# First expert pair of a decoder-trunk kernel: the gather writes its rows already turned, and the gates are turned after the first gate product

## The chip, the cores and the metric

The kernel runs on one core of one Trainium2 chip. The metric is the time in microseconds of one execution on the device, as the median of several runs. TensorE (PE) multiplies and turns tiles, VectorE (DVE) and ScalarE (ACT) do elementwise work, SyncE (SP) issues the large transfers. PE reads its operands from the on-chip memory (SBUF) and writes to PSUM, which has eight banks of 128 partitions x 512 float32 values.

## The reference, cut to what matters

One layer over 320 tokens (256 of a prompt, 64 of samples) with 1024 features. A pooling and a delta-rule mixer are followed by an output projection. Then comes a mixture of 32 experts, of which each token takes four, and it is here that the change lies:

```
h = rmsnorm(x, ln_moe)
logits = h @ router_w + router_b ; top 4 of 32 ; gates = softmax(top_vals)
for each expert e, on the rows of its tokens (xb):
    gt  = minimum(xb @ w_gate[e] + b_gate[e], 7)
    up  = clip(xb @ w_up[e] + b_up[e], -7, 7)
    hid = (up + 1) * (gt * sigmoid(1.702 * gt))
    y   = hid @ w_down[e] + b_down[e]
x[token] += gate * y[slot]
```

A gated per-layer product and a final norm end the layer. Everything is float32; the expert weights are 32 x 3 x 4 MB.

## The kernel before

The five engines run programs of their own, written out by hand and tied by semaphores. Before the experts, PE works through three token tiles (0, 2 and 1 in this order): output projection (L1486), turning of the raw rows (`turn_raw`, L1204), router logits (`logits`, L1504), and ranks of the tokens within each expert (L1584 to L1586 for tiles 0 and 2, bank `rkA`; L1621 to L1623 with all tiles, bank `rkB`). DVE picks the top four (`choose`, L2248 to L2258), makes ranks (L2261), and compares them with a counting row to get the selection matrix `Ssel` (`match_first`, L2265): for each token tile a 128 x 128 matrix of ones and zeros, token by slot, 64 slots for each of the two experts of a pair.

The experts go in 16 pairs. Each pair is three products, gate, up and down (`product`, bias by L1693, weights by L1726), whose weights arrive in 2 MB chunks through a ring of eight slots. The products need the gathered rows with features on the partitions (`xgT`). For the first pair this is made in four steps. `gather_half` (L1594) multiplies with `Ssel` stationary and the normed rows `h3` moving, 512 columns at a time, into banks `ga` and `gb`. ACT copies these to `xg` (L844). PE turns them in eight 128 x 128 pieces (L1204, `ht_region` as source) into banks `xta` and `xtb`. DVE scales these with the norm's weights into `xgT` (`scaled_turn`, L2352). All later pairs have their own gather in bf16 parts (L1567), in the middle of the pair before.

Beside this, DVE multiplies the selection with the gates (`Sgat`, L2347), PE turns the result (three L1204 with `u_region`, bank `sgt`) and ACT copies it out (L1034). `keep_busy` (L1615) issues bias products into an unused bank while PE waits. After the first pair's rows are scaled, DVE works out the table of expert order and overflow blocks (L2357 to L2393), splits the normed rows into three bf16 parts with ACT (L2397, L2400, ACT L1094 and L1097), and only then enters the loop over pairs. There it prepares the next pair's selection (L2316, L2321), takes the gate product out of PSUM (L2450) and marks the experts (`mark_expert`, L2325). PE's gather for the second pair waits for that mark (`pair_sel`).

SP issues a chunk when its ring slot is used up. PE counts these with `chunk_used`. The sequence of SP also waits once for the finished table (L646).

In the trace a float32 product of PE with 128 stationary columns is two MATMUL records, each with a weight load (PEld) of its own. A float32 transpose is one record.

## Time and profile before

| | |
|---|---|
| median of three runs | 1200.1 us (1194.87, 1200.41, 1200.1) |
| span of the profiled execution, first to last instruction | 1196.8 us |
| busy: PE, DVE, ACT | 95%, 34%, 18% |
| data moved | 435.16 MB |

The profile gives the span of its own execution; what lies around the span is not told apart. The median of the runs is 3.3 us above it, and the three runs lie 5.5 us apart. A busy share close to 100% of PE doesn't say that PE sets the end: its records reach over waits for weights.

### The profile page before, as it was taken

Reading aid. Unit: us, or ns where it says so; the run is one execution under the profiler, and the core shown is the slowest. Engines: PE = TensorE matmul, PEld = TensorE weight load, DVE = VectorE, ACT = ScalarE, POOL = GpSimd, SP = SyncE. Lnnn points to the kernel's source line nnn. Section 1 sums busy time; section 2 is a strip of 40 time slices with the busy share of each in tenths; the row PEclk is TensorE's granted clock in tenths of the full one; section 3 lists DMA queues with packets and bytes.
Section 4 is the critical chain, followed back from the end, with each engine's and each line's share of the span. In section 5 each row is a group of like instructions: output and inputs, shape, how many; then the busy total and the mean of one; then the engine's idle time right before and its main releaser. Section 6 shows DMA issues by size and latency. Waiting matters only on the chain.

```text
span 1196.8 us, 15386 instructions
## 1 busy us (share of the span) xinstructions
PE 1141.3 (95%) x5919; PEld 485.4 (41%) x5919; DVE 410.9 (34%) x779; ACT 212.6 (18%) x393; POOL 39.7 (3%) x115
## 2 busy tenths in 40 slices
PE   8999999999999999999999998999999999999997
PEld 5677864433333332333333333333333333332333
DVE  5646764743132222131322231313131313130325
ACT  3434332221111011111010101011110101010025
POOL 6002110000000000000000000000000000000000
PEclk9999999899999999999999999999999999999999
DMA  9911539789999999999999999999999999999931
GB/s 306 292 71 71 167 120 338 266 329 421 429 427 428 426 429 428 424 429 427 428 428 429 427 428 426 428 427 429 425 429 429 428 428 429 428 428 425 419 150 45
DMA packets 50603, 435.16 MB, mean 364 GB/s; under 512 B 6861, under 2 KB 14554, under 8 KB 24812
## 3 DMA queue, kind: packets, MB, share of 16 engines
q1 hardware_dynamic: 44425, 430.22, 87.1%
q10 hardware_dynamic: 6123, 4.18, 1.1%
q8 instruction: 37, 0.61, 0.2%
q14 instruction: 18, 0.15, 0.0%
HBM read 429.54 MB, written 4.11 MB: 362 GB/s over the span
## 4 chain that ended last, share of the span: by engine, by line
PE 70%; DMA 20%; DVE 5%; issue 2%; ACT 2%; POOL 0%; SPq 0%; DVEq 0%; ACTq 0%; POOLq 0%
PE ps L1726 40%; DMA ring<-in_w_gate 13%; DMA ring<-in_w_up 7%; PE ps L1289 7%; PE ps L1672 4%; PE ps L1567 3%; PE ps L1204 3%; PE ps L1486 2%; PE ps L1336 1%; PE ps L1693 1%; PE ps L1403 1%; PE ps L1940 1%; PE ps L1917 1%; DVE x_resid L2426 1%; PE ps L1798 1%
## 5 line engine op out<-in xcount | busy, mean ns | idle before, releaser
L1726 PE MATMUL ps<-ring,ht_region 128*64 128x512 f32 (+1 forms) x2152 | 455.9, 602 | 18.5 <-DMA ring<-in_w_gate 16.4
L1726 PEld LDWEIGHTS ps<-ring,ht_region 128*64 128x64 f32 (+1 forms) x2152 | 149.6, 135 | 309.4 <-issue 309.3
L1726 PE MATMUL ps<-ring,q_region 128*64 128x512 f32 (+1 forms) x1088 | 223.5, 594 | 0.3 <-ACT q_region L844 0.3
L1726 PEld LDWEIGHTS ps<-ring,q_region 128*64 128x64 f32 (+1 forms) x1088 | 71.6, 134 | 144.2 <-issue 143.2
L2426 DVE TENSOR_TENSOR x_resid<-ps,x_resid 128x512 f32<-128x512 f32 (+1 forms) x90 | 62.0, 688 | 148.0 <-PE ps L1672 143.8
L2476 DVE SCALAR_TENSOR_TENSOR q_region<-ps,small,u_region 128x1024 f32<-128x1024 f32 x15 | 19.3, 1283 | 222.9 <-ACT u_region L1076 222.9
L1289 PE MATMUL ps<-ht_region,ring 128*128 128x320 f32 x320 | 89.0, 435 | 1.7 <-DVE ht_region L1979 0.9
L2468 DVE TENSOR_SCALAR q_region<-ps 128x1024 f32<-128x1024 f32 x15 | 18.4, 1225 | 167.2 <-PE ps L1726 167.2
L1289 PEld LDWEIGHTS ps<-ht_region,ring 128*128 128x128 f32 x320 | 59.8, 190 | 27.2 <-issue 3.1
L1054 ACT ACTIVATE q_region<-q_region 128x1024 f32<-128x1024 f32 x16 | 16.9, 1056 | 292.2 <-DVE q_region L2450 292.1
L1672 PE MATMUL ps<-u_region 128*128 128x512 bf16 (+1 forms) x180 | 54.7, 385 | 3.1 <-DVE x_resid L2426 0.4
L1076 ACT ACTIVATE u_region<-ps,small 128x1024 bf16<-128x1024 f32 x15 | 16.7, 1114 | 226.9 <-PE ps L1726 226.9
L1051 ACT ACTIVATE ht_region<-ps 128x512 f32<-128x512 f32 x30 | 17.9, 598 | 210.3 <-PE ps L1567 210.3
L2426 DVE TENSOR_TENSOR ht_region<-ps,vecs 128x512 f32<-128x512 f32 x30 | 20.7, 691 | 49.5 <-PE ps L1204 48.4
L1567 PE MATMUL ps<-z_region,u_region 128*128 128x512 bf16 x90 | 34.3, 381 | 0.3 <-DVE ht_region L2325 0.3
L1567 PE MATMUL ps<-hmid,u_region 128*128 128x512 bf16 x90 | 34.1, 379 | 0.0
L1672 PE MATMUL ps<-z_region,u_region 128*128 128x512 bf16 (+1 forms) x90 | 34.1, 379 | 0.0
L1693 PE MATMUL ps<-bias_s,ht_region 96*128 96x512 bf16 x96 | 28.9, 382 | 2.6 <-ACT lmask L1107 2.6
L1672 PEld LDWEIGHTS ps<-u_region 128*128 128x128 bf16 (+1 forms) x180 | 12.2, 101 | 46.7 <-DVE x_resid L2426 30.0
L1486 PE MATMUL ps<-ring,ht_region 128*128 128x512 f32 x64 | 28.9, 596 | 0.0
L2010 DVE SCALAR_TENSOR_TENSOR h_region<-q_region,vecs,h_region 128x256 f32<-128x256 f32 (+1 forms) x72 | 27.7, 385 | 2.6
L1204 PE MATMUL ps<-ident,q_region 128*128 128x128 f32 x128 | 20.6, 302 | 7.9 <-ACT ht_region L1051 6.9
(489 smaller groups left out, 906.7 us busy)
## 6 DMA issues: line engine op xcount, KB each, us to landing
ring<-in_w_gate SPq DMA_DIRECT2D x62, 2048.0 KB, 25.0
ring<-in_w_up SPq DMA_DIRECT2D x62, 2048.0 KB, 21.9
ring<-in_w_down SPq DMA_DIRECT2D x57, 2048.0 KB, 26.4
ring<-in_w_down SPq DMA_DIRECT2D x13, 1024.0 KB, 24.4
ring<-in_w_in SPq DMA_DIRECT2D x4, 2048.0 KB, 17.5
ring<-in_w_out SPq DMA_DIRECT2D x2, 2048.0 KB, 8.5
ring<-in_w_up SPq DMA_DIRECT2D x4, 1024.0 KB, 25.0
ring<-in_w_ple_gate SPq DMA_DIRECT2D x2, 2048.0 KB, 20.6
```

What stands on the lines that cost most here:

```text
L1051: lstep(a.activation(out, PS[:, b, 0:width], ACT.Copy, **total), drained[b], done)
L1204: return nc.tensor.transpose(out, in_, ident[0:n, 0:n])
L1289: last = mm(ps[:, 0:T], w[:, k, (c % 4) * P:(c % 4 + 1) * P], hT[:, k, :], start=(k == 0), stop=(k == KT - 1))
L1486: last = mm(ps, hT[:, k, t0:t0 + n], wo[k][:, hf * 512:(hf + 1) * 512], start=(k == 0), stop=(k == KT - 1))
L1567: last = mm(ps, Sselb[:, t, :], part(t)[:, hf * 512:(hf + 1) * 512], start=(t == 0 and i == 0), stop=(t == NT - 1 and i == 2))
L1672: last_ = mm(ps[0:n, :], slots_turned[:, t0:t0 + n], y[:, hf * 512:(hf + 1) * 512], start=(part == 0), stop=(part == 2))
L1693: mm(PS[:, b0 + hf, :], ind[:, half, :], biases[bias][:, hf * 512:(hf + 1) * 512], start=True, stop=False, skip_group_check=True)
L1726: ins = mm(PS[s0_:s0_ + width, b0 + hf, :], lhs[:, k, s0_:s0_ + width], rows[:, kk, hf * 512:(hf + 1) * 512], start=False, stop=(k == KT - 1),
L2010: ins = v.scalar_tensor_tensor(out=out, in0=col(j), scalar=vec("conv_w", j * QKV_T + c), in1=out, op0=ALU.mult, op1=ALU.add)
L2426: lmark(op(*args), drained[b], done)
L2468: lmark(v.tensor_scalar(ubuf, PS[:, 2:4, :].rearrange("p b f -> p (b f)"), LIMIT, -LIMIT, ALU.min, ALU.max), up_act, pair + 2)
L2476: lmark(v.scalar_tensor_tensor(out=gbuf, in0=y_psum, scalar=slot_gate[:, half:half + 1], in1=y_hi, op0=ALU.mult, op1=ALU.subtract), yrest, ...
```

## The change

It touches the first pair alone. (1) `gather_half` has the normed rows stationary, 128 columns at a time with a step of four, and `Ssel` moving, and writes straight to `xta` and `xtb`. The banks `ga` and `gb`, the copies by ACT and the eight turns go. (2) The turning of the gates moves from ahead of the first gate product to behind it; ACT's copy of it moves behind the bf16 splits, and PE waits for that copy ahead of the first down product. (3) PE waits for `xta` alone ahead of the gate product and for `xtb` at its second half. (4) DVE compares both experts in one instruction, makes the first pair's `ind` columns ahead of the last ranks, and scales `xta` and `xtb` ahead of the two products for `Sgat`. (5) The second `keep_busy` issues two products in place of four.

```diff
@@ -335,7 +335,6 @@
         h3_zero = sem("h3_zero")
-        h_gathered = sem("h_gathered")
         hi_cast = sem("hi_cast")
@@ -463,7 +462,7 @@
-        for n, b in (("ga", 2), ("gb", 3), ("rT11", 1), ("lg1", 0), ("rkB", 4), ("sgt", 5), ("xta", 6), ("xtb", 7)):
+        for n, b in (("rT11", 1), ("lg1", 0), ("rkB", 4), ("xta", 6), ("xtb", 7), ("sgt", 5)):
             use(n, b)
@@ -1028,12 +1027,6 @@
             exponent(1)
-            for hf, nm in enumerate(("ga", "gb")):
-                copy(xg[:, hf * 512:(hf + 1) * 512], bank(nm), nm)
-            is_filled(act, "sgt")
-            step(a.activation(gates_turned[0], bank("sgt")[:, 0:T], ACT.Copy, accum_out=slot_gate[:, 0:1]),
-                 dsem("sgt"), uses["sgt"][1] + 1)
-
@@ -1089,12 +1082,15 @@
                 if t == 0:
-                    act.wait_ge(h_gathered, 1)
+                    is_filled(act, "xtb")
                     act.wait_ge(chunk_used, half_used(1))
...
                 step(a.activation(h_mid[:, t, :], h3[:, t, :], ACT.Copy), mid_cast)
+            is_filled(act, "sgt")
+            step(a.activation(gates_turned[0], bank("sgt")[:, 0:T], ACT.Copy, accum_out=slot_gate[:, 0:1]),
+                 dsem("sgt"), uses["sgt"][1] + 1)
             turn_body(0, first=True)
@@ -1586,15 +1582,17 @@
-            first_banks = [fill("ga"), fill("gb")]
+            first_banks = [fill("xta"), fill("xtb")]
...
                 n = TILES[t][1]
-                last = mm(first_banks[hf], Ssel[0:n, t, :], h3[0:n, t, hf * 512:(hf + 1) * 512],
-                          start=(t == ORDER[0]), stop=(t == ORDER[-1]), skip_group_check=True)
+                for kk in range(RPP):
+                    c0 = hf * RPP * P + kk
+                    last = mm(first_banks[hf][:, kk * P:(kk + 1) * P], h3[0:n, t, c0:(hf + 1) * RPP * P:RPP], Ssel[0:n, t, :],
+                              start=(t == ORDER[0] and kk == 0), stop=(t == ORDER[-1]), skip_group_check=True)
                 if t == ORDER[-1]:
-                    last.then_inc(fsem(("ga", "gb")[hf]), 1)
+                    last.then_inc(fsem(("xta", "xtb")[hf]), 1)
@@ -1612,7 +1610,7 @@
                 for _ in range(n):
-                    mm(bank("xta"), onesb[0:3 * E, :], bias3[:, 0:512], start=True, stop=True)
+                    mm(bank("op10"), onesb[0:3 * E, :], bias3[:, 0:512], start=True, stop=True)
@@ -1622,24 +1620,18 @@
             last.then_inc(fsem("rkB"), 1)
-            keep_busy(4)
+            keep_busy(2)
             pe.wait_ge(v_mark, VM["ssel1"])
...
             gather_rows(1)
-            for hf, nm in enumerate(("ga", "gb")):
-                is_drained(pe, nm)
-                ps = fill(("xta", "xtb")[hf])
-                c0 = hf * RPP * P
-                for k in range(4):
-                    last = tr(ps[:, k * P:(k + 1) * P], xg[:, c0 + k:c0 + RPP * P:RPP])
-                last.then_inc(fsem(("xta", "xtb")[hf]), 1)
-            pe.wait_ge(bias_ready, 16 * 12)
-            pe.nop().then_inc(h_gathered, 1)
-            pe.wait_ge(v_mark, VM["sgat"])
-            ps = fill("sgt")
-            for t in range(NT):
-                last = tr(ps[:, t * P:(t + 1) * P], Sgat[:, t, :])
-            last.then_inc(fsem("sgt"), 1)
+
+            def turn_first_gates():
+
+                pe.wait_ge(v_mark, VM["sgat"])
+                ps = fill("sgt")
+                for t in range(NT):
+                    last = tr(ps[:, t * P:(t + 1) * P], Sgat[:, t, :])
+                last.then_inc(fsem("sgt"), 1)
@@ -1683,6 +1675,9 @@
+                            if first and half == 0:
+                                is_drained(pe, "xta")
+                                return
                             for b in (6, 7):
@@ -1707,6 +1702,8 @@
                                     pe.wait_ge(early_in, 16)
+                                if first and half == 0 and bias == 0 and c == 2:
+                                    is_drained(pe, "xtb")
                                 for kk, hf in (LATE_HALF if final and bias == 2 and c > c0 else IN_ROWS):
@@ -1742,6 +1739,8 @@
                         product(0, 0, xgT, 0, rows_turned)
+                        if first and half == 0:
+                            turn_first_gates()
@@ -1773,6 +1772,8 @@
                                 ins.then_inc(fsem(f"pT{k}"), 1)
+                        if first and half == 0:
+                            is_drained(pe, "sgt")
                         product(2 * CPM, 4, hidT, 2)
@@ -2261,9 +2262,10 @@
-            def match_first(t, e):
-                return v.tensor_scalar(Ssel[:, t, e * CAP:(e + 1) * CAP], iotaf[:, 1:CAP + 1], rank[:, e, t:t + 1], None,
-                                       ALU.is_equal)
+            def match_first(t):
+                return v.tensor_tensor(Ssel[:, t, :].rearrange("p (e s) -> p e s", e=2),
+                                       iotaf[:, 1:CAP + 1].unsqueeze(1).broadcast_to([P, 2, CAP]),
+                                       rank[:, 0:2, t].unsqueeze(2).broadcast_to([P, 2, CAP]), ALU.is_equal)
@@ -2290,8 +2292,8 @@
             drain(ranks(2, bank("rkA")[:, E:2 * E]), "rkA")
-            step(match_first(0, 0)), step(match_first(0, 1)), step(match_first(2, 0))
-            mark(match_first(2, 1), "ssel02")
+            step(match_first(0))
+            mark(match_first(2), "ssel02")
             add_half(1, 1)
@@ -2299,10 +2301,12 @@
             choose(1)
+            for a_ in range(2):
+                step(v.tensor_copy(ind[:, 0, a_ * CAP:(a_ + 1) * CAP], ident3[:, a_:a_ + 1].broadcast_to([3 * E, CAP])),
+                     pair_sel if a_ else None)
             is_filled(dve, "rkB")
             step(ranks(1, bank("rkB")[:, 0:E]))
-            step(match_first(1, 0))
-            mark(match_first(1, 1), "ssel1")
+            mark(match_first(1), "ssel1")
             drain(v.tensor_copy(cnt, bank("rkB")[:, E:2 * E]), "rkB")
@@ -2333,8 +2337,6 @@
-            match, weigh, mark_expert = select(0, (0, 1))
-            step(mark_expert(0)), step(mark_expert(1), pair_sel)
             dve.wait_ge(a_mark, AM["exq1"])
@@ -2342,15 +2344,14 @@
                                  den.unsqueeze(2).broadcast_to([P, NT, E]), ALU.mult))
+            for nm, k0 in (("xta", 0), ("xtb", 4)):
+                is_filled(dve, nm)
+                drain(v.tensor_tensor(*scaled_turn(bank(nm), k0)), nm)
             for a_ in range(2):
...
                 mark(ins, "sgat") if a_ else step(ins)
-            for nm, k0 in (("xta", 0), ("xtb", 4)):
-                is_filled(dve, nm)
-                drain(v.tensor_tensor(*scaled_turn(bank(nm), k0)), nm)
-            is_filled(dve, "sgt")
@@ -2484,6 +2485,7 @@
+            is_filled(dve, "sgt")
             turn_body(0, first=True)
```

In the rows below, those of PE stand ahead of the first gate product, from the last `keep_busy` on. `bias_s,onesb` is `keep_busy`, `h_region,u_region` is the gather with `h3` moving, `ident,ht_region` the turn of `xg`, `ident,u_region` that of the gates. Before:

```order
L1615 MATMUL ps<-bias_s,onesb 128x512 x4
L1594 MATMUL ps<-h_region,u_region 128x512 [waits a_mark,v_mark]
L1594 MATMUL ps<-h_region,u_region 128x512
L1204 MATMUL ps<-ident,ht_region 128x128 [waits drained6,drained2]
L1204 MATMUL ps<-ident,ht_region 128x128 x3
L1204 MATMUL ps<-ident,ht_region 128x128 [waits drained7,drained3]
L1204 MATMUL ps<-ident,ht_region 128x128 x3
L1204 MATMUL ps<-ident,u_region 128x128 [waits bias_ready,drained5,v_mark]
L1204 MATMUL ps<-ident,u_region 128x128 x2
L1693 MATMUL ps<-bias_s,ht_region 128x512 [waits drained3,drained2,drained4,drained1,h3_zero,drained0,g_act,pair_sel]
L1693 MATMUL ps<-bias_s,ht_region 128x512
L1726 MATMUL ps<-ring,ht_region 64x512 [waits chunk_in1,chunk_in0,early_in,drained7,drained6]
```

After:

```order
L1613 MATMUL ps<-bias_s,onesb 128x512 x2
L1592 MATMUL ps<-u_region,h_region 128x128 [waits a_mark,v_mark]
L1592 MATMUL ps<-u_region,h_region 128x128 x7
L1688 MATMUL ps<-bias_s,ht_region 128x512 [waits drained3,drained2,drained4,drained1,h3_zero,drained0,g_act,pair_sel]
L1688 MATMUL ps<-bias_s,ht_region 128x512
L1723 MATMUL ps<-ring,ht_region 64x512 [waits chunk_in1,early_in,chunk_in0,drained6]
```

The gather has four times as many instructions of a quarter of the columns, with the operands exchanged, and the three groups of turns between it and the bias products are gone.

The gates' turn stands on PE between the first gate product (its last rows, from `q_region` and `ring`) and the bias of the first up product. After:

```order
L1723 MATMUL ps<-ring,ht_region 64x512
L1723 MATMUL ps<-q_region,ht_region 64x512
L1200 MATMUL ps<-ident,u_region 128x128 [waits drained5,v_mark]
L1200 MATMUL ps<-ident,u_region 128x128 x2
L1688 MATMUL ps<-bias_s,ht_region 128x512 [waits up_act,y_act]
L1688 MATMUL ps<-bias_s,ht_region 128x512
```

Its wait is now for a product of DVE made long before, and the up product comes behind it.

On DVE, from behind the last tile's comparison to the start of the table (`hmid<-hmid,iotaf`). Before:

```order
L2325 CAST ht_region<-ident 96x64 [waits drained4]
L2325 CAST ht_region<-ident 96x64 [waits v_step]
L2339 TENSOR_TENSOR hmid<-hmid,selb 128x96 [waits a_mark,pair_sel]
L2340 TENSOR_REDUCE hmid<-hmid 128x3 [waits v_step]
L2341 TENSOR_SCALAR hmid<-hmid 128x3 [waits v_step]
L2342 RECIPROCAL hmid<-hmid 128x3 [waits v_step]
L2343 TENSOR_TENSOR gate<-hmid 128x3x32 [waits v_step]
L2347 TENSOR_TENSOR u_region<-u_region,gate 128x3x64 [waits v_step] x2
L2352 TENSOR_TENSOR ht_region<-ps,vecs 128x512 [waits filled6,v_mark]
L2352 TENSOR_TENSOR ht_region<-ps,vecs 128x512 [waits filled7,drained6]
L2357 SCALAR_TENSOR_TENSOR hmid<-hmid,iotaf 128x32 [waits ssm_stored,filled5,drained7]
```

After, from that comparison (now one instruction) on:

```order
L2266 TENSOR_TENSOR u_region<-iotaf,rank 128x128 [waits v_step]
L2310 COPY hmid<-ps 128x32 [waits v_mark]
L2341 TENSOR_TENSOR hmid<-hmid,selb 128x96 [waits a_mark,drained4]
L2342 TENSOR_REDUCE hmid<-hmid 128x3 [waits v_step]
L2343 TENSOR_SCALAR hmid<-hmid 128x3 [waits v_step]
L2344 RECIPROCAL hmid<-hmid 128x3 [waits v_step]
L2345 TENSOR_TENSOR gate<-hmid 128x3x32 [waits v_step]
L2349 TENSOR_TENSOR ht_region<-ps,vecs 128x512 [waits filled6,v_step]
L2349 TENSOR_TENSOR ht_region<-ps,vecs 128x512 [waits filled7,drained6]
L2352 TENSOR_TENSOR u_region<-u_region,gate 128x3x64 [waits drained7]
L2352 TENSOR_TENSOR u_region<-u_region,gate 128x3x64 [waits v_step]
L2358 SCALAR_TENSOR_TENSOR hmid<-hmid,iotaf 128x32 [waits ssm_stored,v_mark]
```

The two casts (`mark_expert`) are gone from here to a place ahead of the last ranks, and the two `u_region<-u_region,gate` products (`Sgat`) went behind the two scalings (`ht_region<-ps,vecs`), which the table follows.

## Rows read from the trace of the kernel before

**Rows 1.** The page: the span, and the transfer rate in 40 slices.

```profile
span 1196.8 us, 15386 instructions
...
GB/s 306 292 71 71 167 120 338 266 329 421 429 427 428 426 429 428 424 429 427 428 428 429 427 428 426 428 427 429 425 429 429 428 428 429 428 428 425 419 150 45
```

**Rows 2.** The chain in order of time, late in the span: start, us, what.

```profile
658.27 29.42 DMA ring<-in_w_gate
```

**Rows 3.** Busy time by stretch; the last two columns are DMA share and GB/s.

```profile
218.00:225.00 7.00, 6.85 (x28) 3.18 (x28) 4.12 (x16) 1.72 (x4) 0.00 (x0) 0.82 0.03 12
...
266.00:270.00 4.00, 4.00 (x22) 1.41 (x20) 0.00 (x0) 0.00 (x0) 0.00 (x0) 1.00 0.58 184
270.00:1140.00 870.00, 834.13 (x3962) 298.92 (x3961) 224.12 (x325) 94.49 (x139) 0.00 (x0) 0.99 1.01 427
```

**Rows 4.** PE in order of time, 205 to 223 us: start, us, what, idle before.

```profile
205.37 1.96 PE L1486 MATMUL ps<-ring,ht_region 128*128 128x512 f32 x4
207.64 1.10 PE L1594 MATMUL ps<-h_region,u_region 128*128 128x512 f32 x2 [0.31 <-issue]
208.57 0.60 PE L1204 MATMUL ps<-ident,x_resid 128*128 128x128 f32 x4
...
211.94 2.10 PE L1594 MATMUL ps<-h_region,u_region 64*128 64x512 f32 x4
213.98 1.04 PE L1615 MATMUL ps<-bias_s,onesb 96*128 96x512 bf16 x2
...
215.02 1.87 PE L1615 MATMUL ps<-bias_s,onesb 96*128 96x512 bf16 x4
216.68 3.62 PE L1594 MATMUL ps<-h_region,u_region 128*128 128x512 f32 x4
220.09 1.71 PE L1204 MATMUL ps<-ident,ht_region 128*128 128x128 f32 x8
221.63 0.49 PE L1204 MATMUL ps<-ident,u_region 128*128 128x128 f32 x3
222.09 0.59 PE L1693 MATMUL ps<-bias_s,ht_region 96*128 96x512 bf16 x2
222.70 0.61 PE L1726 MATMUL ps<-ring,ht_region 128*64 128x512 f32 x1
```

**Rows 5.** The same view: a float32 product and a strided turn of this shape.

```profile
175.33 1.05 PE L1336 MATMUL ps<-q_region 128*128 128x128 f32 x8
...
256.28 1.22 PE L1204 MATMUL ps<-ident,q_region 128*128 128x128 f32 x8 [0.52 <-ACT ht_region L1051]
```

**Rows 6.** Stretches of 1 us; the column ahead of the last two is the granted clock.

```profile
213.00:214.00 1.00, 1.00 (x4) 0.12 (x3) 0.86 (x5) 0.21 (x1) 0.00 (x0) 0.84 1.00 426
...
220.00:221.00 1.00, 0.91 (x5) 0.62 (x3) 0.00 (x0) 0.60 (x1) 0.00 (x0) 0.75 0.00 0
```

**Rows 7.** DVE in order of time.

```profile
206.10 1.12 DVE L2265 TENSOR_SCALAR u_region<-iotaf,rank 128x64 f32<-128x64 f32 x4
207.44 0.69 DVE L2220 TENSOR_TENSOR x_resid<-ps,x_resid 128x512 f32<-128x512 f32 x1 [0.21 <-PE ps L1486]
...
215.52 0.55 DVE L2265 TENSOR_SCALAR u_region<-iotaf,rank 128x64 f32<-128x64 f32 x2
...
218.09 0.75 DVE L2347 TENSOR_TENSOR u_region<-u_region,gate 128x192 f32<-128x192 f32 x2
...
221.90 0.69 DVE L2352 TENSOR_TENSOR ht_region<-ps,vecs 128x512 f32<-128x512 f32 x1 [0.20 <-PE ps L1204]
222.63 0.19 DVE L2357 SCALAR_TENSOR_TENSOR hmid<-hmid,iotaf 128x32 f32<-128x32 f32 x1
...
247.46 0.36 DVE L2316 TENSOR_TENSOR u_region<-iotaf,rank 128x192 bf16<-128x192 f32 x1 [1.59 <-issue]
```

**Rows 8.** ACT in order of time, the second copy of the gathered rows.

```profile
220.40 0.60 ACT L844 ACTIVATE ht_region<-ps 128x512 f32<-128x512 f32 x1 [1.11 <-PE ps L1594]
```

**Rows 9.** PE in order of time, at the second pair's gather.

```profile
251.38 0.39 PE L1567 MATMUL ps<-z_region,u_region 128*128 128x512 bf16 x1 [0.30 <-DVE ht_region L2325]
```

## The prediction

> **What bounds the kernel now.** I read the page first: from slice 10 on, the transfer rate stands at 417 to 430 GB/s to the end of the weights [rows 1]. The stretches say the same: full from 270 us to 1140 us at 427 GB/s, half idle at 266 to 270 us and all but idle at 218 to 225 us [rows 3]. Late in the span the chain of work runs for 29.42 us at a time through transfers of weights [rows 2]: PE has used up what the ring held and waits. So the last two thirds of the kernel go at the pace of the transfers. Nothing in the change moves a byte, and it can bring only as much as the stream as a whole starts earlier. The stream is not full until 270 us because its issues wait for ring slots, which PE frees in the first pair. What counts is when PE does the first pair's products, above all the down product behind [rows 9], which frees the slots whose refill ends the last hole.
>
> Next I read PE, DVE and ACT in order of time, from 205 us to the first product and on to the second pair's gather. Here PE has hardly a gap, but much of what it does on the way is there to wait: from 220.09 us, where PE is through with the gather's columns, a chain runs over the tail of the last record (ACT starts 0.31 us later), ACT's copy of 0.60 us [rows 8], four turns, and DVE's scaling, to the first weight product at 222.70 us [rows 4]. That is 2.61 us from 220.09 us. The other chain is DVE's. It starts the expert table at 222.63 us [rows 7] and has work without a pause until it marks the second pair. PE comes to its gather at 251.38 us after 0.30 us of waiting for DVE [rows 9]. **So two chains end together there, PE's at 251.08 us and DVE's at 251.38 us, and a gain counts only as far as both move.**
>
> **Ahead of the last tile.** Four comparisons of 64 columns take 1.12 us, and PE stands 0.31 us ahead of its first gather [rows 4, 7]. Two comparisons of 128 columns: one of 64 is 0.28 us, one of 192 is 0.36 us [rows 7]; I take 0.32 us, so the pair takes 0.64 us plus a little and the gather starts up to 0.4 us earlier. The turns of the raw rows behind it wait for DVE's add, which ends at 208.13 us either way [rows 7], so of their 208.57 us only 0.2 us can go. The bounds are 0 and 0.4 us.
>
> **The gather with its operands exchanged.** Before, one tile and half is two records of 512 columns, and the next work of PE starts 0.93 us after the first (207.64 to 208.57 us, the opening load included [rows 4]); the last tile's records, at half clock, are 0.85 us apart, so at full clock a record is 0.43 us. Now it is four products of two records, 128 columns each. The same view has both sides of the price: eight records of such a product with whole rows stationary take 1.05 us in all, of which 0.28 us is the last one's own length: 0.77 / 7 = 0.11 us a record. Eight turns with stationary columns four apart, as here, take 1.22 us with one break among them, likewise at most 0.94 / 7 = 0.13 us a record [rows 5]. I take 0.12 us, so 0.96 us for eight records, where two old ones took 0.86 us (bounds 0.89 and 1.07 us). The streamed columns are the same number, and only the weight loads could show. The first tile's second half lies under a wait for DVE's copy and costs nothing; should that cover go, it is 0.1 us. Tile 2, 16 records, goes to 1.92 us; before, 211.94 to 213.98 us is 2.04 us, since the clock halves in the last 0.3 us of it (granted clock 0.84 over 213 to 214 us, level 1.2 in place of 2.4 GHz) [rows 4, 6]. PE had products and loads without a gap over 0.31 us before it fell [rows 4]. Started 0.2 us earlier, the tile ends at 213.66 us, 0.3 us earlier.
>
> The Trainium skill (TensorE: Matmul & The Clock Gate, "The mechanism") says that a weight load overlaps with a product in flight only when it goes to other row groups. By that, all 48 loads of the new form would stand in the open and the time would be that of the third rival below; by the rows it stays as summed here. The eight contiguous records disagree, since 0.11 us holds nothing beyond the streaming; the strided ones come near it.
>
> **The last tile.** The two `keep_busy` products and the ranks keep their length, so the ranks are in PSUM 0.3 us earlier. DVE's selection was ready at 216.07 us (215.52 plus 0.55 us [rows 7]); now one comparison of 0.32 us in place of 0.55 us gives 215.54 us. DVE's two casts went ahead of the ranks, into a wait of DVE for PE; if that wait were gone they would cost some 0.4 us. PE issued four fillers from 215.02 us and came to the gather at 216.68 us, 1.66 us for four; two take 0.83 us from 214.72 us, so the selection now decides, and the gather starts at about 215.65 us, **1.0 us earlier**. At half clock it took 216.68 to 220.09 us, 3.41 us [rows 4]. The same columns stream at the same clock, and a record of 0.21 us hides the load better than one of 0.11 us: again 3.41 us, ending at 219.06 us.
>
> **From the gather to the products.** Four turns a half, ACT's copies and a DVE step drop out of the chain. `xta` is filled halfway through the gather, and DVE, through with the gates by then, scales it in 0.69 us under the other half. PE goes on with the two bias products, 0.83 us at half clock (by the fillers), and the weight product starts at about 219.9 us in place of 222.70 us. Until the clock is back at 220.5 us (granted clock 0.75 over 220 to 221 us [rows 6]) it does 0.3 us of work in 0.6 us. In work done PE is 2.5 us ahead. The turn of the gates, 221.63 to 222.09 us, 0.46 us [rows 4], is now behind the gate product and comes back: PE reaches the second gather **2.0 us earlier**, at 249.05 us. `xtb` is needed at the gate product's second half, 7 us in, and is there. ACT's copy of the turned gates stands behind the splits and is wanted only at the down product, many us later: nothing. The moved turn frees no slot and moves no transfer; behind it in PE's queue is the up product, which loses its 0.46 us, counted above.
>
> **DVE.** `xtb` is filled 0.31 us behind the gather's last column, as the old bank was [rows 4, 8]: 219.06 + 0.31 = 219.37 us. Scaling 0.69 us, then the two products for `Sgat`, 0.75 us [rows 7], which before lay hidden under the waiting, and the table starts at about 220.85 us with its step between instructions: **1.75 us earlier** than 222.63 us. What follows is the same work, the next pair's selection included, and SP's wait for the table moves with it. So DVE releases the gather at 251.38 − 1.75 = 249.63 us, after PE's 249.05 us; PE waits 0.6 us there in place of 0.30 us, and DVE's number counts.
>
> **Sum.** The second gather and all behind it, the down product, the slots, and the stream from its last hole on, come 1.75 us earlier, and the end with them. The profiled span of 1196.8 us [rows 1] becomes 1195.05 us. The median of the runs shown, 1200.1 us, is 3.3 us above that span; I take this as what lies around it and carry it over: 1198.3 us. The three runs lie 5.5 us apart, so a measurement of this kernel can hardly tell less than 0.5%, 6 us, from no change.
>
> **The rivals.**
> *The clock stays up.* The fall at 213.68 us follows the logits and a gather of 64 rows, and the change gives PE other records there. Without it the fillers, ranks and last gather (213.98 to 220.09 us, 5.0 us of it streaming) would shrink: the selection would come at about 214.8 us, the gather end at 216.8 us and the table start at 218.6 us: 4 us earlier, 1196.1 us. For it speaks only that every gather record now has a load beside it; against it, that the stretch before the fall stays nearly as it was.
> *The clock stays down longer.* The gather streams ones and zeros from `Ssel` where it streamed the rows. If the half clock lasts 3.4 us longer (as long as half the present stay), PE loses 1.7 us in the products, arrives only 0.3 us earlier, and the end is 1199.8 us.
> *The other side: strided loads don't hide.* If each of the 48 records showed its load for 0.1 us or more beyond my 0.12 us, the 40 that lie on the path cost 4 us and the end is 1202.4 us. It decides from 1.75 / 40 = 0.044 us a record on. The strided turns' 0.13 us at most speaks against it; but those streamed an identity with one record to a turn.
> *Nothing passes on.* If the stream's full part doesn't shift with the first pair, because its last hole is closed by something else, 1200.1 us. Against it: the hole at 266 to 270 us is PE's slots.
>
> **How the numbers follow.** Forecast 1198.3 us, its own range 1197.4 to 1199.2 us, 0.58. Clock up 0.12, clock down longer 0.12, nothing passes on 0.12, loads in the open 0.06. All centres but the last lie between 1196.1 and 1200.1 us; the medians' own spread adds some 3 to 4 us on the lower side, where one of the three runs lay, and 2 on the upper: 1192.5 to 1202 us. Faster by over 0.5% needs 1194.1 us, beyond even the clock case, and can come only together with low runs: 0.15. Slower by over 0.5% needs 1206.1 us: 0.04. Within: 0.81.
>
> **What would show it.** PE: 48 gather records, 0.12 us apart at full clock and 0.21 us at half; gather of the last tile from 215.6 to 219.1 us; first weight product at about 219.9 us; three turns behind the gate product; 0.6 us of waiting for DVE at the second gather at 249.6 us. DVE: table from 220.9 us. Stream: the hole at 266 us at 264.3 us. Wrong would be a granted clock that falls at another time, records over 0.16 us apart, or an end that doesn't follow the second gather.

## The result, and the profile after

The changed kernel takes **1202.04 us** (median of 20 runs, 1199.08 to 1206.02), the kernel before 1198.59 us (20 runs beside it, 1194.08 to 1204.77). The ratio is 1.0031, interval 1.0020 to 1.0043: slower by 0.3%, where 1198.3 us and a ratio of 0.9985 were forecast. By the forecast's own bound of 0.5% this is "within"; the sign is the other one, and the time is that of the rival "strided loads don't hide", which had 0.06. One run of them all (of e9 below, 1218.53 us) was in a slow state and counts in no ratio and no mean.

The profiled execution took 1206.02 us. The page of the changed kernel:

```profile
span 1204.5 us, 15429 instructions
...
GB/s 318 252 95 70 166 114 285 257 358 375 425 427 427 428 428 428 428 426 428 428 427 430 427 427 426 427 430 428 429 427 429 429 429 427 427 428 426 419 152 45
```

What lies around a span is therefore 1.5 us, not the 3.3 us taken from the median; with it the profiled execution of before took 1198.3 us, not 1200.1 us. The span is 7.7 us longer than in [rows 1], but most of that is no work of the change. PE in order of time, from where the rows of [rows 4] begin to the second gather of [rows 9]:

```profile
210.70 1.96 PE L1482 MATMUL ps<-ring,ht_region 128*128 128x512 f32 x4
212.50 1.92 PE L1592 MATMUL ps<-u_region,h_region 128*128 128x128 f32 x8
...
214.69 2.03 PE L1592 MATMUL ps<-u_region,h_region 128*128 128x128 f32 x8
...
218.35 4.10 PE L1592 MATMUL ps<-u_region,h_region 64*128 64x128 f32 x16
...
223.42 1.01 PE L1613 MATMUL ps<-bias_s,onesb 96*128 96x512 bf16 x2
224.27 4.10 PE L1592 MATMUL ps<-u_region,h_region 128*128 128x128 f32 x16
228.17 0.91 PE L1688 MATMUL ps<-bias_s,ht_region 96*128 96x512 bf16 x2
229.00 0.64 PE L1723 MATMUL ps<-ring,ht_region 128*64 128x512 f32 x1
...
242.89 0.55 PE L1200 MATMUL ps<-ident,u_region 128*128 128x128 f32 x3
...
258.98 0.39 PE L1563 MATMUL ps<-z_region,u_region 128*128 128x512 bf16 x1 [1.23 <-DVE ht_region L2329]
```

The first row stood at 205.37 us in [rows 4]. Nothing ahead of it was changed, and over the 18 profiles of this study it stands anywhere from 205.37 us to 210.70 us (the changed kernel again, in e10: 208.84 us). From here on I count all times from this record, which takes those 5.33 us out. Then the first weight product starts at 18.3 us in place of 17.3 us, and the second gather at 48.3 us in place of 46.0 us, 2.3 us later. A late gather record is what [rows 5] did not show: 16 of them take 4.10 us, and single ones lie 0.233 us apart.

DVE in order of time, which answers to [rows 7]:

```profile
211.44 0.62 DVE L2266 TENSOR_TENSOR u_region<-iotaf,rank 128x128 f32<-128x128 f32 x2
...
226.61 0.69 DVE L2349 TENSOR_TENSOR ht_region<-ps,vecs 128x512 f32<-128x512 f32 x1 [0.84 <-PE ps L1592]
228.48 0.69 DVE L2349 TENSOR_TENSOR ht_region<-ps,vecs 128x512 f32<-128x512 f32 x1 [1.17 <-PE ps L1592]
229.21 0.75 DVE L2352 TENSOR_TENSOR u_region<-u_region,gate 128x192 f32<-128x192 f32 x2
229.99 0.19 DVE L2358 SCALAR_TENSOR_TENSOR hmid<-hmid,iotaf 128x32 f32<-128x32 f32 x1
```

DVE waits for the gather twice, 0.84 and 1.17 us, and the table starts at 19.3 us in place of 17.3 us. Stretches of 1 us and of the stream, the answers to [rows 6] and [rows 3]:

```profile
218.00:219.00 1.00, 1.00 (x7) 0.96 (x6) 0.42 (x2) 0.85 (x3) 0.00 (x0) 0.77 0.96 410
...
228.00:229.00 1.00, 1.00 (x4) 0.25 (x3) 0.52 (x1) 0.00 (x0) 0.00 (x0) 0.61 0.07 16
229.00:230.00 1.00, 1.00 (x7) 0.43 (x8) 0.90 (x4) 0.00 (x0) 0.00 (x0) 1.00 0.00 0
272.00:280.00 8.00, 8.00 (x40) 2.59 (x37) 0.00 (x0) 0.00 (x0) 0.00 (x0) 1.00 0.65 246
280.00:1140.00 860.00, 824.29 (x3883) 295.84 (x3883) 223.98 (x325) 93.94 (x138) 0.00 (x0) 0.99 1.01 427
```

The clock falls about where it did but stays down 10.2 us (218.5 to 228.8 us), where it was 6.8 us. The stream is full again from 280 us, at the same 427 GB/s. The last expert weight product starts 941.6 us from the counted record, before 939.3: in this pair of profiles the 2.3 us of the second gather are there at the end.

### The profile page after: what moved, and what is told of

The parts are those of the page before. It is cut to its first block, busy times and chain, and to the rows that moved or that the text cites. A ratio compares the mean times of both kernels' runs of the same rounds, so it can differ in the third digit from the quotient of the medians.

```text
span 1204.5 us, 15429 instructions
## 1 busy us (share of the span) xinstructions
PE 1148.9 (95%) x5945; PEld 496.0 (41%) x5945; DVE 410.8 (34%) x776; ACT 211.5 (18%) x391; POOL 39.2 (3%) x115
## 4 chain that ended last, share of the span: by engine, by line
PE 67%; DMA 21%; DVE 6%; ACT 2%; issue 2%; SPq 1%; POOL 0%; DVEq 0%; ACTq 0%; POOLq 0%
PE ps L1723 40%; DMA ring<-in_w_gate 18%; PE ps L1285 7%; PE ps L1664 4%; PE ps L1563 3%; DMA ring<-in_w_up 2%; PE ps L1200 2%; PE ps L1482 2%; PE ps L1332 2%; PE ps L1688 1%; DVE x_resid L2427 1%; PE ps L1918 1%; PE ps L1592 1%; SPq L604 1%; PE ps L1473 1%
## 5 line engine op out<-in xcount | busy, mean ns | idle before, releaser
L1723 PE MATMUL ps<-ring,ht_region 128*64 128x512 f32 (+1 forms) x2152 | 456.1, 603 | 18.3 <-DMA ring<-in_w_gate 17.8
L2477 DVE SCALAR_TENSOR_TENSOR q_region<-ps,small,u_region 128x1024 f32<-128x1024 f32 x15 | 19.3, 1284 | 222.9 <-ACT u_region L1069 222.9
L2469 DVE TENSOR_SCALAR q_region<-ps 128x1024 f32<-128x1024 f32 x15 | 18.4, 1225 | 165.6 <-PE ps L1723 165.5
L2427 DVE TENSOR_TENSOR ht_region<-ps,vecs 128x512 f32<-128x512 f32 x30 | 20.8, 692 | 49.5 <-PE ps L1200 48.4
## 6 DMA issues: line engine op xcount, KB each, us to landing
ring<-in_w_gate SPq DMA_DIRECT2D x62, 2048.0 KB, 24.6
ring<-in_w_up SPq DMA_DIRECT2D x62, 2048.0 KB, 21.8
```

Of the source, the lines that this page charges most:

```text
L1723: ins = mm(PS[s0_:s0_ + width, b0 + hf, :], lhs[:, k, s0_:s0_ + width], rows[:, kk, hf * 512:(hf + 1) * 512], start=False, stop=(k == KT - 1),
L2427: lmark(op(*args), drained[b], done)
L2469: lmark(v.tensor_scalar(ubuf, PS[:, 2:4, :].rearrange("p b f -> p (b f)"), LIMIT, -LIMIT, ALU.min, ALU.max), up_act, pair + 2)
L2477: lmark(v.scalar_tensor_tensor(out=gbuf, in0=y_psum, scalar=slot_gate[:, half:half + 1], in1=y_hi, op0=ALU.mult, op1=ALU.subtract), yrest, ...
```

## The experiments

Times of the middle columns are counted from the same record, in each kernel's one profile: "last gather" is the first gather record of the last tile, "product" the first weight product, "table" the start of DVE's table, "2nd gather" the second pair's, with what PE waited for it. "Clock down" is how long the clock was down in this stretch; "half clock" is the mean over a kernel's timed runs of the whole time at 1.2 GHz, from each run's granted clock as 2 x (1 - clock) x time. Each ratio is to the kernel before on the same chip.

| kernel | ratio, interval | median us | last gather | product | table | 2nd gather (PE waits) | clock down | half clock |
|---|---|---|---|---|---|---|---|---|
| before | 1 | 1198.59 | 11.3 | 17.3 | 17.3 | 46.0 (0.3) | 6.8 | 21.2 |
| changed | 1.0031 (1.0020, 1.0043) | 1202.04 | 13.6 | 18.3 | 19.3 | 48.3 (1.2) | 10.2 | 26.9 |
| e1 | 0.9984 (0.9968, 1.0000) | 1195.69 | 9.9 | 12.3 | 13.7 | 43.0 (1.9) | none | 18.9 |
| e2 | 0.9981 (0.9964, 0.9999) | 1196.49 | 9.9 | 12.3 | 13.7 | 43.0 (1.9) | none | 20.3 |
| e3 | 0.9998 (0.9981, 1.0015) | 1198.39 | 10.3 | 16.3 | 17.3 | 46.5 (1.5) | 6.8 | 21.8 |
| e5 | 1.0031 (1.0012, 1.0050) | 1201.82 | 13.7 | 17.2 | 18.5 | 47.5 (1.5) | 6.8 | 28.2 |
| e6 | 1.0011 (0.9992, 1.0031) | 1198.26 | 10.3 | 15.2 | 16.0 | 45.0 (1.1) | 6.8 | 24.2 |
| e7 | 1.0026 (1.0005, 1.0046) | 1201.60 | 13.7 | 18.4 | 19.4 | 47.1 (0) | 10.2 | 27.2 |
| e8 | 0.9970 (0.9950, 0.9990) | 1195.40 | 11.0 | 15.0 | 16.2 | 43.7 (0) | 6.8 | 22.7 |
| e9 | 1.0030 (1.0010, 1.0049) | 1199.65 | 12.9 | 15.3 | 16.6 | 45.9 (1.8) | none | 21.4 |
| e10 | 1.0032 (1.0015, 1.0050) | 1200.98 | 13.6 | 18.3 | 19.3 | 48.6 (1.5) | 10.2 | 25.6 |
| e11 | 1.0005 (0.9985, 1.0025) | 1199.07 | 10.2 | 14.6 | 14.5 | 43.1 (0.2) | none | 22.4 |
| e12 | 0.9986 (0.9970, 1.0001) | 1194.70 | 10.2 | 13.3 | 14.6 | 42.3 (0.2) | 3.4 | 21.3 |
| e13 | 1.0029 (1.0011, 1.0046) | 1201.11 | 13.7 | 18.0 | 19.1 | 48.4 (1.7) | 6.8 | 26.6 |
| e14 | 1.0018 (0.9998, 1.0037) | 1200.39 | 12.9 | 15.3 | 16.6 | 45.9 (1.8) | none | 21.4 |
| e15 | 0.9996 (0.9975, 1.0017) | 1196.81 | 9.9 | 12.5 | 13.7 | 42.9 (1.7) | none | 24.2 |
| e16 | 0.9997 (0.9975, 1.0018) | 1198.37 | 9.9 | 12.3 | 13.7 | 42.9 (1.8) | none | 24.6 |

(Before's half clock is that of 134 runs beside e1, e5, e10 and e16; the means of these four sets are 23.3, 21.3, 18.4 and 22.2 us.)

**e1 and e16: contiguous columns.**

```diff
-                    c0 = hf * RPP * P + kk
+                    c0 = hf * RPP * P + kk * P
-                    ... h3[0:n, t, c0:(hf + 1) * RPP * P:RPP], Ssel[0:n, t, :],
+                    ... h3[0:n, t, c0:c0 + P], Ssel[0:n, t, :],
```

> The changed kernel, with the normed rows' stationary columns taken 128 side by side instead of four apart (the first pair's rows then come out with their features in another order, so the first pair multiplies them with the wrong weight rows; the same instructions otherwise). Theory A, the strided weight load is what costs: a record falls from 0.233 us to about 0.11 us at full and 0.21 us at half clock; from the first record of the last four of the output projection to the start of the expert table it takes about 15.5 to 16.5 us (19.29 us changed, 17.26 us before), the second pair's gather follows that, and the time is 0.1 to 0.2% under the kernel before (ratio 0.998 to 0.999). Theory B, the longer stay at half clock costs, whatever the loads do: the records get shorter at full clock, but the half clock still stands for 10 us and the time stays at a ratio of 1.001 to 1.003. Theory C, the first pair passes nothing on to the end: the ratio stays 1.003 whatever the first pair does.

> All gather columns contiguous (first pair's features in a mixed order), again, on this chip: 5 us less than the strided-early kernel, mean half clock 19 to 21 us; ratio to the kernel before 0.998.

PE of e1 in order of time:

```profile
207.18 1.10 PE L1592 MATMUL ps<-u_region,h_region 128*128 128x128 f32 x8
...
211.75 2.05 PE L1592 MATMUL ps<-u_region,h_region 64*128 64x128 f32 x16
...
215.31 2.05 PE L1592 MATMUL ps<-u_region,h_region 128*128 128x128 f32 x16 [0.39 <-DVE u_region L2266]
217.20 0.60 PE L1688 MATMUL ps<-bias_s,ht_region 96*128 96x512 bf16 x2
```

Same instructions, same count, only the addresses differ: at full clock 8 records take 1.10 us where the changed kernel's took 1.92 us. The last tile's 16 take 2.05 us in place of 4.10 us, but there the clock is another one too (up here, down in the changed kernel). The loss is gone. e16 had the same profile but a ratio of 0.9997: what contiguous columns bring over the kernel before is between 0 and 0.2%. Of what e16 expected, neither the half clock (24.6 us, not 19 to 21) nor the distance to the kernel with strided early columns (2.7 us by the medians of e13 and e16, not 5) came out.

**e2: the same for a full computation.** ScalarE writes the normed rows in permuted order, so that the gather's columns are contiguous and the rows still have their features in order; the gather's lines change as in e1, and later pairs' turns take contiguous columns too.

```diff
-                step(a.activation(h3[0:n, t, :], x3[0:n, t, :], ACT.Copy, ...
+                step(a.activation(h3[0:n, t, :].rearrange("t (h k p) -> t h k p", h=2, k=RPP),
+                                  x3[0:n, t, :].rearrange("t (h p k) -> t h k p", h=2, k=RPP), ACT.Copy, ...
```

> The whole computation, with the normed rows written by ScalarE in the order in which they are wanted, so that the gather's stationary columns lie side by side; the later pairs' rows then are turned from columns side by side too. Theory A: as the run with contiguous columns, ratio 0.998 to 0.999, ScalarE's write of a tile stays near 1.15 us. If ScalarE's read with a step of four floats is slow (over 2 us a tile), the last gather's start may come later by the excess less 4 us of slack, that is not at all below 5 us. Theory B: ratio 1.001 to 1.003. Theory C: 1.003.

It stands as e1 does, 0.9981. ScalarE pays for it; one tile's rows in order of time:

```profile
214.37 2.12 ACT L997 ACTIVATE h_region<-x_resid,small 128x1024 f32<-128x1024 f32 x1 [0.66 <-DVE small L2313]
```

In the changed kernel it is 1.15 us. PE still comes to the last gather when it does in e1, at 9.9 us, so slack hides the 1 us.

**e3: the old gather, with the rest of the change.** Selection, copies and turns as before; one comparison, the moved turn of the gates and DVE's new order stay. The fillers write into a bank that the old gather uses, so the first pair's rows are overwritten.

```diff
-                for kk in range(RPP): ...
+                last = mm(first_banks[hf], Ssel[0:n, t, :], h3[0:n, t, hf * 512:(hf + 1) * 512], ...
```

> The gather, the copies by ScalarE and the turns as before; the rest of the change kept (gates turned behind the gate product, one comparison per tile, marks ahead of the ranks, scalings ahead of the gate products, two fillers). Theory A: no strided loads, so the time lies near or under the kernel before; the last gather starts about 1.0 us earlier, PE reaches the second pair's gather 1.4 us earlier but DVE, with the gate products now behind the scalings, only about 0.25 us, so the ratio is 0.999 to 1.000. Theory B and a rival of A, the moved gates and the order on DVE are what costs: the ratio is 1.002 to 1.003.

0.9998 (0.9981 to 1.0015): the rest is worth nothing that can be measured. The whole loss is the new gather's.

**e4: the operand forms by themselves.** Ahead of the first gate product of the kernel before stand eight products or turns of each float32 form and sixteen of each bf16 form, into an unused bank; nobody uses their results. It ran once, and its time plays no part.

```diff
+            for _ in range(8):
+                mm(pr, hp[:, 0:P], sp_, start=True, stop=True)          # L1651
+            for _ in range(8):
+                mm(pr, hp[:, 0:2 * P:2], sp_, start=True, stop=True)    # L1653
...
```

The columns are 1, 2, 4 and 8 floats apart (L1651 to L1657), then the streamed operand 4 apart (L1659), float32 turns 1 and 4 apart (L1661, L1663), and bf16 with 2 and 8 bytes (L1665, L1667).

> The kernel before, with nine groups of products and turns put ahead of the first gate product that write to an unused bank and change nothing else: eight float32 products each with stationary columns at steps 1, 2, 4 and 8, eight with the moving columns at a step of 4, eight turns each at steps 1 and 4, sixteen bf16 products each with stationary columns at steps 1 and 4. Theory A: at full clock a float32 record takes 0.11 us at step 1 and 0.23 us at step 4; if the load's time goes by the distance, step 2 lies between and step 8 above; if any step halves the rate, steps 2, 4 and 8 are all 0.23 us. A turn, whose load is 0.14 us long at step 1 and 0.21 us at step 4, stays at 0.11 to 0.12 us. A moving operand at a step of 4: 0.11 us if the moving side reads strided columns at full rate. The rival, that the one-hot moving operand or PSUM accumulation slowed the gather: step 4 with the identity moving stays at 0.11 us.

PE in order of time:

```profile
223.21 1.95 PE L1651 MATMUL ps<-ident,h_region 128*128 128x128 f32 x16
225.00 2.05 PE L1653 MATMUL ps<-ident,h_region 128*128 128x128 f32 x16
226.88 3.89 PE L1655 MATMUL ps<-ident,h_region 128*128 128x128 f32 x16
230.62 3.97 PE L1657 MATMUL ps<-ident,h_region 128*128 128x128 f32 x16
234.42 3.82 PE L1659 MATMUL ps<-h_region,ident 128*128 128x128 f32 x16
238.06 1.06 PE L1661 MATMUL ps<-ident,h_region 128*128 128x128 f32 x8
238.96 1.13 PE L1663 MATMUL ps<-ident,h_region 128*128 128x128 f32 x8
239.92 1.06 PE L1665 MATMUL ps<-onesb,bias_s 96*128 96x128 bf16 x16
240.82 1.06 PE L1667 MATMUL ps<-onesb,bias_s 96*128 96x128 bf16 x16
```

Single records lie 0.112, 0.118, 0.233 and 0.238 us apart at steps 1, 2, 4 and 8. In a product, two floats to 16 bytes are read at full rate, one at half. With the streamed operand strided it is 0.228 us, so either side's reading can set the pace. bf16 columns 8 bytes apart cost nothing (0.056 us).

A turn with step 4 takes only 0.120 us a record. It has a load to each record as a product has, and at step 1 its records lie as far apart (0.109 us); what differs is the load, by the records of the weight loads (least, median and greatest duration in ns):

```profile
L1651 PEld LDWEIGHTS ps<-ident,h_region x16: 190/192/192, 223.1 to 224.8; 128*128 128x128 f32 x16
L1655 PEld LDWEIGHTS ps<-ident,h_region x16: 308/330/330, 226.8 to 230.3; 128*128 128x128 f32 x16
L1661 PEld LDWEIGHTS ps<-ident,h_region x8: 139/140/161, 237.8 to 238.7; 128*128 128x128 f32 x8
L1663 PEld LDWEIGHTS ps<-ident,h_region x8: 196/211/212, 238.8 to 239.7; 128*128 128x128 f32 x8
```

The stride lengthens a product's load by 0.14 us and a turn's by 0.07 us. Why a turn's load is the shorter one, no run shows. So [rows 5] could not give the price of a strided product.

The Trainium skill (SBUF — State Buffer, "Specifications (TRN2)"; Advanced Engine Details and Errata, "SBUF Cachelines") says that the memory is read in lines of 16 bytes, and that two hits on a line are needed for the full rate. The seven product forms agree with it: slow at 16 and 32 bytes, on either side, and not at 8 or below. The turn at 16 bytes has the longer load, but next to nothing of it shows in its pace. The rule speaks against this change and was not weighed in the prediction.

**e15: step two in the kernel.** `h3[0:n, t, c0:c0 + 2 * P - 1:2]` in all 48 records.

> All 48 gather records with every second column, 8 bytes apart, in place of every fourth (first pair's features in a mixed order). The probe had 0.118 us a record at this step: 48 records at 0.118 us, time as with contiguous columns, 1195 to 1197 us. Rival, the probe's small loop does not carry over, and the form is slow here as at step four: 1201 us or more.

Its last gather, first product and table are e1's within 0.1 us, and 1196.81 us. The boundary lies between 8 and 16 bytes in the kernel too.

**e5, e13 and e6: strided in one place alone.** In e5 and e13 tiles 0 and 2 (32 records) stay strided and the last tile (16) is contiguous; e6 is the reverse.

```diff
+                    rows_ = h3[0:n, t, c0:(hf + 1) * RPP * P:RPP]
+                    if t == ORDER[-1]:                      # e6: if t != ORDER[-1]
+                        c0 = hf * RPP * P + kk * P
+                        rows_ = h3[0:n, t, c0:c0 + P]
```

> The changed kernel with the last tile's 16 gather records taken from contiguous columns of the rows; the 32 records of tiles 0 and 2 stay strided (leaves the first pair's features in a mixed order, so that pair's result is another). Theory: a strided record is 0.233 us apart from the next at either clock, a contiguous one 0.11 us at full and 0.21 us at half clock. Two cases are told apart. If the slow records ahead of it bring the longer half clock (10.2 us in the changed kernel's profile), the last gather still runs at half clock and its records are 0.21 us apart: the product starts only some 0.3 us earlier than in the changed kernel, and the time is within 0.5 us of its 1202.0 us. If the half clock has no tie to them, the last gather goes at 0.11 us a record and the product starts 1.9 us earlier or more: about 1200.0 us. Rival, cost by place: all that was lost was lost in the last tile, where nothing covers it: then 1198 us or less.

> The changed kernel with the 32 gather records of tiles 0 and 2 taken from contiguous columns and the last tile's 16 left strided (leaves the first pair's features in a mixed order). Theory: the selection for the last tile is there 10.0 us behind the first ranks, as with all columns contiguous, and the last gather takes 3.7 us in place of 1.8 us at 0.233 us a record; the end is 1.9 us behind the all-contiguous kernel's 1195.7 us: 1197.6 us, and the clock does not fall ahead of the gather. Rival, the clock falls whatever the form of the early records: gather starts 10 to 11 us behind the ranks but product some 3 us later still: 1199 to 1200 us.

> The kernel with strided columns in tiles 0 and 2 and contiguous ones in the last tile (first pair's features in a mixed order), again, beside the next three on one chip: 1201 to 1202 us, mean time at half clock 26 us or more. It is the reference for the tie between slow reading and clock.

The last gather of e6, at half clock, strided:

```profile
217.67 4.10 PE L1596 MATMUL ps<-u_region,h_region 128*128 128x128 f32 x16
```

and that of e8 (described below), at half clock, contiguous:

```profile
218.41 3.62 PE L1603 MATMUL ps<-u_region,h_region 128*128 128x128 f32 x16
```

Single strided records lie 0.233 us apart at half clock here as at full clock in the changed kernel's first tile (212.50 us, 1.92 us for 8). From the first record's start to the last one's it is 3.66 us; contiguous, it is 3.35 us at half clock (e8) and 1.78 us at full (e1). So the last tile's loads cost 0.3 us if the clock is down and up to 1.9 us if it is not, and **most of the loss lies in tiles 0 and 2**: the last gather starts at 13.7 us in e5 and at 10.3 us in e6. e5 has the whole ratio, 1.0031 (e13 again: 1.0029), as the first case of its expectation has it. Its product comes 1.1 us and not 0.3 us earlier, because the clock came back at 16.0 us, under the last gather. e6 forecast a clock that stays up; it fell, and the time lies between both of its cases.

**e9 and e14: as long, but at full rate.** Contiguous columns, and the 32 early records each issued twice.

```diff
+                    if t != ORDER[-1]:
+                        mm(bank("op10")[:, 0:P], h3[0:n, t, c0:c0 + P], Ssel[0:n, t, :], start=True, stop=True)
```

> The changed kernel with contiguous gather columns throughout (first pair's features in a mixed order) and each of the 32 records of tiles 0 and 2 issued twice, once into an unused bank. Two full-rate records take 0.22 us, about what one strided record takes (0.233 us), so PE is held as long as by the strided ones but reads twice the columns. Theory A, only the length counts: last gather starts some 13.5 us behind the first ranks, the end and the time at half clock are those of the kernel with strided columns in tiles 0 and 2 (1201.8 us, 28 us at half clock in the mean of its runs). Theory B, the slow reading itself goes with more time at half clock: the start of the last gather is the same 13.5 us, but the mean time at half clock is that of the contiguous kernel, 19 to 21 us, and the time 3 us less, about 1199 us.

> Contiguous columns with the 32 early records issued twice (first pair's features in a mixed order), again, beside the strided one. If only the length counts, time and half clock are those of the strided kernel less 0.8 us of last-gather start. If the slow reading goes with more time at half clock, the mean is 4 us or more below the strided kernel's, and the time 2 us below.

PE is held to 12.9 us, nearly as long as in e5, with every record at full rate. The ratios are 1.0030 and 1.0018, those of e5 and e13 1.0031 and 1.0029. **So holding PE that long is enough for most of the loss, if not for all of it**: what costs is that a strided record takes twice the time, and no further harm of slow reading has to be assumed.

The clock is another matter. Stretches of 16 us from the same place in the program, the changed kernel first:

```profile
217.00:233.00 16.00, 16.00 (x77) 11.13 (x78) 8.88 (x37) 2.25 (x6) 0.00 (x0) 0.68 0.46 185
```

and e9:

```profile
213.00:229.00 16.00, 15.75 (x110) 10.14 (x110) 10.66 (x48) 5.29 (x8) 0.00 (x0) 1.00 0.60 236
```

The granted clock (third column from the right) is 0.68 and 1.00. Over all timed runs the doubled form was 21.4 us at half clock (23 runs, standard error 1.3), as the kernel before (21.2, error 0.6, 134 runs) and the other full-rate forms (e1, e2, e8, e12, e15, e16: 22.0, error 0.7, 72 runs); the kernels with strided early records, the changed one among them, 26.9 us (error 0.5, 68 runs). So slow reading went with 5 us more at half clock, and records of about the same length at full rate did not. That is an association and not a mechanism: the profiles of e5 and e13 show 6.8 us in this stretch like that of before, so where their other half clock lies is open, and beside e13 (26.6 us) stood contiguous e16 with 24.6 us. In time it is less: e13 is 0.7 us above e14 on one chip, e5 and e13 together 1.4 us above e9 and e14 in the mean, with a standard error of 0.7 us, and 0.9 us of it is the later start of the last gather. The 2 us that e14 expected, if slow reading goes with more half clock, were not seen. Half clock costs little where the strided records lie, as they take 0.233 us at either.

**e7, e8, e11, e12: DVE's chain made shorter.** The overflow table compares 19 x 64 columns twice with the same result; made once, one of its six steps of 1.4 us goes (the expectation of e7 calls them twelve). e7 does so in the changed kernel, e8 and e12 in e2, e11 in the kernel before.

```diff
+            step(v.tensor_tensor(is_block, pos.unsqueeze(1).broadcast_to([P, OV_MAX, 64]), ..., ALU.is_equal))
             for src, dst in ((evec, ove_f), (ovec, ov_off[:, :])):
-                step(v.tensor_tensor(cmp_, pos.unsqueeze(1)..., ALU.is_equal))
-                step(v.tensor_tensor(cmp_, cmp_, src...
+                step(v.tensor_tensor(cmp_, is_block, src...
```

> The changed kernel in full, with one of DVE's twelve long steps in the overflow table gone: the comparison of 19 x 64 columns, made twice for the same numbers, is made once into the space of the gathered rows; DVE's chain to the second pair's mark is 1.4 us shorter, and nothing of PE's is touched. If DVE is what the second gather waits for, as the wait of 1.23 us there says, the gather and the end come 1.2 us earlier, PE's own time being the bound from there: 1200.8 us against the changed kernel's 1202.0 us. Rival, the wait at the gather is not passed on to the stream's slots: no change.

> The kernel with the normed rows written in permuted order, contiguous gather columns, and the same single comparison in DVE's overflow table (a full computation). PE waited 1.85 us for DVE at the second gather; 1.4 us of it should go: 1195.1 us against the permuted kernel's 1196.5 us, ratio to the kernel before 0.997. Rival, the end does not follow the second gather by less than 2 us: 1196.5 us as it was.

> The kernel before in full with DVE's overflow comparison made once in place of twice, nothing else. PE waits for DVE only 0.30 us at its second gather, so PE's chain is next: 0.3 us earlier there, ratio to the kernel before 0.9998, and no wait of PE left. Rival: the shorter DVE chain is worth its whole 1.4 us (ratio 0.9988), and the permuted kernel with it owes its gain to that alone.

> The full computation with permuted rows, contiguous gather columns and the single comparison, again, on the chip of the other three: ratio to the kernel before 0.997 as measured, and 5 to 6 us less than the changed kernel. Rival: the first measurement was a low one, and it comes out within 0.1% of the kernel before.

At the second gather of e7 and of e8 PE waits for nothing any more; of e7:

```profile
254.66 0.39 PE L1563 MATMUL ps<-z_region,u_region 128*128 128x512 bf16 x1
```

In e7 the gather comes 1.2 us earlier than in the changed kernel (47.1 against 48.3 us), as expected: DVE was what it waited for. The medians, 1201.6 and 1202.0 us, can't tell 1.2 us. e8 and e12 are the fastest of the study, 1195.40 and 1194.70 us, 0.9970 and 0.9986, some 0.2% below the kernel before and some 6 us below the changed one on the same chips (e7, e10); e11 shows no such gain (1.0005), but its interval (0.9985 to 1.0025) holds theirs. That the shorter chain pays only with the contiguous gather is therefore not shown; e8 lies 1.1 us below e2, which the intervals do not tell from nothing.

**e10: the changed kernel again.**

> The changed kernel as it is, beside the others on one chip: 1202 us, mean time at half clock 27 us a run, and in the profile a half clock of 10.2 us from 8 us behind the first ranks if that belongs to it; rival: a stay of 6.8 us as in most other profiles, the longer one being chance.

1.0032, and the same profile: down for 10.2 us. All three profiles with all 48 records strided (changed, e7, e10) have that length; none of the other 15 has over 6.8 us in this stretch.

## Why the prediction was wrong

**The step that failed** is the price of a gather record: "I take 0.12 us", with bounds of 0.11 and 0.13 us [rows 5]. It is 0.233 us, beyond the 0.16 us that the prediction named as a sign of being wrong. The upper bound came from turns, whose load is short even when strided (0.21 us against a product's 0.33 us in e4); the lower from products with whole rows. Neither row was a strided product, and the two properties together are what costs. A bound that no row excluded was a load wholly in the open: the strided turns' own load records take 0.21 us in the kernel before, and the third rival counted with a price near it.

```profile
L1204 PEld LDWEIGHTS ps<-ident,q_region x8: 197/209/221, 256.2 to 257.1; 128*128 128x128 f32 x8
```

"The same columns stream at the same clock" failed likewise: the reading, not the streaming, sets the pace, and does so at either clock.

**What the step moved.** The last gather starts 2.3 us later (13.6 against 11.3 us) where 1.0 us earlier was forecast: 3.3 us, from 32 records at 0.11 us more each, less what lies under DVE's copy. The last tile adds 0.3 us to the forecast 3.4 us. The first product is at 18.3 us (forecast 14.5), the table at 19.3 us (forecast 15.5), the second gather at 48.3 us (forecast 44.3): some 4 us all the way.

**What was right.** Comparisons of 128 columns at 0.31 us (forecast 0.32). The first tile's gather starts 0.5 us earlier from the counted record, just past the bound of 0.4. The selection decides the last gather's start, and it comes 1.0 us earlier once the early records are contiguous and the clock falls as before: e6, 10.3 against 11.3 us. The turn of the gates stands behind the gate product at 0.4 us. DVE and not PE decides at the second gather (a wait of 1.23 us, forecast 0.6; e7 confirms it). A shift there reaches the end: in this pair 2.3 us and 2.3 us. Over the other profiles the last weight product moves with the second gather, but only within 1 to 2 us: e9 and e14 have the gather at 45.9 us both and that product at 936.8 and 938.6 us; e7 has 47.1 and 939.1 us, before 46.0 and 939.3 us. So the equal 2.3 us are in part luck. With records at full rate the forecast of 1.75 us less is within what was measured (e1, e2, e15, e16: 0.9981 to 0.9997, that is 0.4 to 2.3 us less). With the clock up in both it is smaller: the table of e16 against e11, 13.7 and 14.5 us, is 0.8 us earlier, since turns and copies that the change removes are shorter too.

**The rivals.** "Strided loads don't hide" happened, at 0.11 us beyond the price taken, two and a half times its threshold of 0.044 us. That its 1202.4 us missed by only 0.4 us is luck in part: its base was over 1.5 us too high, and it had the change 2.3 us slower than before, where the medians have 3.45 us. "The clock stays down longer" happened with it, by the 3.4 us it names, but not for the reason given (ones and zeros streamed; the contiguous kernels stream them too). "The clock stays up" is what the profiles with every record at full rate show in six of eight cases (e1, e2, e9, e14, e15, e16, not e8 and e12), but so does e11 with the old gather. "Nothing passes on" is refuted.

**Between profile and medians.** The profiles differ by 2.3 us from the counted record on, the medians by 3.45 us. The rest fits the clock: before's profile had the fall of 6.8 us, while its runs were at half clock 5.7 us less than the changed kernel's in the mean, and a profile of the old gather without the fall (e11) has its table 2.8 us earlier. That is argued from single profiles, not shown. A reading of the rate row was slightly off as well: the row has 419 to 429 GB/s from slice 10 on, not 417 to 430 [rows 1]; nothing hangs on it.

**The forecast's base** was 1.5 to 1.8 us too high (1200.1 us for a profiled execution of 1198.3 us and a median of 1198.59 us), so that its 1198.3 us lies where the kernel before does. In the difference of the kernels it missed by 1.75 + 3.45 = 5.2 us, in the time by 3.7 us.

## What to carry to other kernels

Price an operand by its bytes: if neighbouring float32 columns of a product's operand lie 16 bytes or more apart, count twice the time for each record (0.233 against 0.112 us here); a turn did not pay it (0.120 us). Take a bound only from a row that has all the properties of the new form together. And where the layout is free, let the engine that writes the rows permute them: here ScalarE did it in 2.1 us a tile in place of 1.15 us, under other work, and the gather lost its penalty.

## What the runs showed that I had not expected

- Reading one float in 16 bytes halves the rate of a product for the stationary operand (0.233 us) and for the streamed one (0.228 us) alike, and the record takes 0.233 us at 2.4 and at 1.2 GHz.
- Weight loads of the same rows do hide behind a product in flight: the 16 records of eight float32 products with contiguous columns (L1651 above) lie 0.112 us apart, though each load record is 0.192 us long, and a record of 512 columns takes 0.43 us: nothing is left beyond the streaming. The Trainium skill (TensorE: Matmul & The Clock Gate, "The mechanism") says otherwise for loads to the same row group; with contiguous columns the profiles here (e1, e2, e8, e12, e16 and L1651) disagree.
- PE busy throughout, but held by slow reading, went with 5 us more at half clock; doubled records of full rate did not. Why is open, and in time the two differ by 0.7 us on one chip and 1.4 us in the mean of both pairs (standard error 0.7 us).
- ScalarE reading floats 16 bytes apart takes 2.12 to 2.14 us for 1024 columns where 1.15 us is usual.
